# Gate weights stacked in one tile, and attention probabilities scaled on GpSimd instead of VectorE, in a one-core transformer layer

## What is computed

```python
def hybrid_mixer(x, w_in, conv_w, conv_b, ig_b, fg_b, ml_g, w_out, rel_table):
    proj = x @ w_in
    qa, ka, va, qk_m, vm, om, gates = jnp.split(proj, SPLITS, axis=-1)
    att = dilated_attention(heads(qa, 8), heads(ka, 8), heads(va, 8), rel_table)
    ig = (gates[..., :ML_HEADS] + ig_b).transpose(0, 2, 1)
    fg = (gates[..., ML_HEADS:] + fg_b).transpose(0, 2, 1)
    h = mlstm(heads(qm, 4), heads(km, 4), heads(vm, 4), ig, fg)
    ...
    return jnp.concatenate([att, h], axis=-1) @ w_out

# in the attention, per head and per block of 128 queries
logits = q @ k.T * ATT_HD ** -0.5 + bias      # masked outside the band
p = jnp.exp(logits - max(logits))
o = (p @ v) / sum(p)
```

## Time and profile before

| | |
|---|---|
| median of three runs | 1164.14 us |
| time of the profiled execution | 1164.95 us |
| its span, first to last instruction | 1163.0 us |
| TensorE busy | 99% |
| TensorE weight loads busy | 82% |
| VectorE busy | 49% |
| ScalarE busy | 36% |
| GpSimd busy | 3% |
| the chain that ended last | TensorE 97%, VectorE 2%, ScalarE 1% |
| TensorE's granted clock | 1.00 of full speed |

### The profile page before, as it was taken

One profiled execution on the slowest core, in us unless ns is written; L12 is line 12 of the kernel. 1 busy time (PEld: TensorE's weight loads), 2 busy tenths in 40 slices (PEclk: granted clock), 3 DMA queues, 4 the chain that ended last, 5 costly groups with the idle time before them and its releaser, 6 DMA issues.

```text
span 1163.0 us, 14755 instructions
## 1 busy us (share of the span) xinstructions
PE 1150.1 (99%) x5490; PEld 958.7 (82%) x5490; DVE 573.1 (49%) x930; ACT 422.2 (36%) x688; POOL 32.7 (3%) x49
## 2 busy tenths in 40 slices
PE   9999999999999999999999999999999999999997
PEld 8888888888888777888798888789888888888886
DVE  3533333343328588765884864456433333343325
ACT  4412212233225377643463454444221222233222
POOL 3000000000001011000000000000000000000000
PEclk9999999999999999999999999999999999999999
DMA  7532222232222222242243241232322222232211
GB/s 282 212 104 95 90 105 93 90 122 95 91 90 73 91 75 82 81 152 85 73 160 112 93 149 67 73 109 91 127 92 107 90 95 104 90 123 95 91 36 73
DMA packets 33563, 120.85 MB, mean 104 GB/s; under 512 B 3900, under 2 KB 3916, under 8 KB 33264
## 3 DMA queue, kind: packets, MB, share of 16 engines
q1 hardware_dynamic: 30528, 109.07, 27.3%
q0 software_dynamic: 2992, 11.19, 2.8%
HBM read 118.13 MB, written 2.11 MB: 103 GB/s over the span
## 4 chain that ended last, share of the span: by engine, by line
PE 97%; DVE 2%; ACT 1%; issue 0%; DVEq 0%; POOL 0%; POOLq 0%
PE ps L446 31%; PE ps L448 30%; PE ps L447 30%; PE ps L463 1%; PE ps L668 1%; PE ps L689 1%; PE ps L740 1%; PE ps L756 1%; PE ps L661 0%; PE ps L597 0%; PE ps L660 0%; DVE lg L1536 0%; PE ps L850 0%; DVE qs L1493 0%; DVE lg L1544 0%
## 5 line engine op out<-in xcount | busy, mean ns | idle before, releaser
L1336 DVE TENSOR_TENSOR wlo<-raw,whi 128x1024 fp32r<-128x1024 f32 x196 | 240.0, 1228 | 373.0 <-ACT whi L911 371.9
L446 PE MATMUL ps<-xth,whi 128*128 128x512 f32 (+1 forms) x924 | 355.0, 384 | 0.0
L448 PE MATMUL ps<-xth,wlo 128*128 128x512 f32 (+1 forms) x924 | 353.0, 382 | 0.0
L447 PE MATMUL ps<-xtl,whi 128*128 128x512 f32 (+1 forms) x924 | 352.9, 382 | 0.0
L911 ACT ACTIVATE whi<-raw 128x1024 fp32r<-128x1024 f32 (+1 forms) x204 | 207.1, 1037 | 152.1 <-PE ps L448 142.8
L448 PEld LDWEIGHTS ps<-xth,wlo 128*128 128x128 f32 x924 | 173.7, 188 | 34.1
L447 PEld LDWEIGHTS ps<-xtl,whi 128*128 128x128 f32 x924 | 173.8, 188 | 32.9
L446 PEld LDWEIGHTS ps<-xth,whi 128*128 128x128 f32 x924 | 173.8, 188 | 32.4
L446 PE MATMUL ps<-whi,hhi 128*128 128x512 f32 x480 | 187.8, 391 | 0.0
L448 PE MATMUL ps<-whi,hlo 128*128 128x512 f32 x480 | 186.9, 389 | 0.0
L447 PE MATMUL ps<-wlo,hhi 128*128 128x512 f32 x480 | 186.8, 389 | 0.0
(11 more groups left out here) (186 smaller groups left out, 997.2 us busy)
## 6 DMA issues: line engine op xcount, KB each, us to landing
raw<-in_units SPq DMA_DIRECT2D x204, 512.0 KB, 3.3
gb<-in_ln_g POOLq DMA_DIRECT2D x4, 512.0 KB, 3.9
gb<-in_ln_b POOLq DMA_DIRECT2D x4, 512.0 KB, 5.4
xn<-in_x POOLq DMA_DIRECT2D x4, 512.0 KB, 12.0
wb<-in_bias_by_key POOLq DMA_DIRECT2D x8, 256.0 KB, 3.0
out<-xn SPq DMA_DIRECT2D x8, 256.0 KB, 2.1
gsp<-g_rows POOLq DMA_DIRECT2D x1, 1024.0 KB, 4.8
memn<-in_mem_cols POOLq DMA_DIRECT2D x1, 1024.0 KB, 8.1
```

What stands on the lines that cost most here:

```text
L446: mm(dst, lh, rh, start=start, stop=False)
L447: mm(dst, lh, rl, start=False, stop=False)
L448: return mm(dst, ll, rh, start=False, stop=stop)
L1336: v.tensor_tensor(wlo[c % SPL][:, :], raw[c % RAW][:, :], whi[c % SPL][:, :].bitcast(F32), ALU.subtract).then_inc(lo_done, 1)
```

## The change

It has four parts. The gate weights go into one tile `wg` of 100 columns per block, high parts in columns 0 to 35 and low parts in columns 64 to 99, and the gate rows are formed with two matmuls per block (by `xh` and by `xl`) instead of three. The low part's rows come out as rows 64 to 99 of the same bank, so ScalarE copies two more 4 x 512 tiles out, and VectorE adds them in. The tile lies where `vx` lies, so `vx` is set to ones later, after the gate rows. The multiplication of the probabilities moves from VectorE to GpSimd, with a new semaphore `rinv_done` between the reciprocal and it. VectorE's `split(U_QK + 5)` moves behind the key's low parts. And `mem_key(0)` waits for the two pieces of `mtl` one by one.

```diff
-        wg_hi = at("wg_hi", [P, KT, GW], ...)
-        wg_lo = at("wg_lo", [P, KT, GW], ...)
+        wg = at("wg", [P, KT, 64 + GW], ar + 82 * KB, F32R)
...
@@ GpSimd
-            nc.gpsimd.memset(vx[:, :, :, :], 1.0).then_inc(pool_ok, 1)
+            nc.gpsimd.memset(wg[:, :, :].bitcast(F32), 0.0).then_inc(pool_ok, 1)
...
+            pool.wait_ge(grow_ready, 1)
+            nc.gpsimd.memset(vx[:, :, :, :], 1.0).then_inc(pool_ok, 1)
             pool.wait_ge(rows_done, 1)
             pool.dma_start(g_rows, grow[:, :]).then_inc(g_out, 16)
-            for h in range(2, AH):
-                bias_in(h)
-                bias_masked(h)
+
+            def scale_p(n):
+
+                w = (n % NB + 1) * P
+                pool.wait_ge(rinv_done, n + 1)
+                nc.gpsimd.tensor_scalar(lg[n % 3][:, 0:w], lg[n % 3][:, 0:w], rinv[:, n:n + 1], None, ALU.mult)\
+                    .then_inc(p_scaled, 1)
+
+            for n in range(NA):
+                if n % NB == NB - 1 and n // NB + 2 < AH:
+                    bias_in(n // NB + 2)
+                scale_p(n)
+                if n % NB == 0 and 2 <= n // NB + 1 < AH:
+                    bias_masked(n // NB + 1)
@@ TensorE
-                last = three(ps[1][0:GW, :], wg_hi[:, k, :], wg_lo[:, k, :], xh[:, k, :], xl[:, k, :], k == 0, k == KT - 1)
+                mm(ps[1][0:64 + GW, :], wg[:, k, :], xh[:, k, :], start=k == 0, stop=False)
+                last = mm(ps[1][0:64 + GW, :], wg[:, k, :], xl[:, k, :], start=False, stop=k == KT - 1)
...
-                    pe.wait_ge(mlo_done, 2)
...
-                cols_part(U_XK + t, ps[6 + t % 2][:, 0:MB * P], mth, mtl, 0, KT)
+                for half in range(2):
+                    if t == 0:
+                        pe.wait_ge(mlo_done, half + 1)
+                    cols_part(U_XK + t, ps[6 + t % 2][:, 0:MB * P], mth, mtl, 4 * half, 4 * half + 4)
@@ ScalarE
             fn(r_f[:, :], ps[1][32:GW, :], ACT.Copy).then_inc(f_ready, 1)
+            fn(r_e[:, :], ps[1][96:64 + GW, :], ACT.Copy).then_inc(f_ready, 1)
+            fn(r_a[:, :], ps[1][64:64 + MH, :], ACT.Copy).then_inc(f_ready, 1)
@@ VectorE
-            step.link(v.tensor_scalar(r_f[:, :], r_f[:, :], gbias[:, 1:2], None, ALU.add))
+            step.link(v.scalar_tensor_tensor(out=r_f[:, :], in0=r_f[:, :], scalar=gbias[:, 1:2], in1=r_e[:, :],
+                                             op0=ALU.add, op1=ALU.add))
...
-            split(U_QK + 5)
             k_lo(0, 0)
             k_lo(0, 1)
+            split(U_QK + 5)
...
-            def scale_p(n):
-                w = (n % NB + 1) * P
+            def invert_sum(n):
                 dve.wait_ge(p_done, n + 1)
-                step.link(v.reciprocal(rinv[:, n:n + 1], rsum[:, n:n + 1]))
-                v.tensor_scalar(lg[n % 3][:, 0:w], lg[n % 3][:, 0:w], rinv[:, n:n + 1], None, ALU.mult)\
-                    .then_inc(p_scaled, 1)
+                v.reciprocal(rinv[:, n:n + 1], rsum[:, n:n + 1]).then_inc(rinv_done, 1)
```

More of the change, by code:

```diff
@@ L213, in macaron_layer @@
         grow = at("grow", [MH, S], ar + 82 * KB + NB * MH * (P + 1) * 4)
-        wg_hi = at("wg_hi", [P, KT, GW], ar + 82 * KB + NB * MH * (P + 1) * 4, F32R)
-        wg_lo = at("wg_lo", [P, KT, GW], ar + 82 * KB + NB * MH * (P + 1) * 4 + KT * GW * 4, F32R)
+        wg = at("wg", [P, KT, 64 + GW], ar + 82 * KB, F32R)
         mth = at("mth", [P, KT, MB * P], ar + 32 * KB, F32R)
@@ L287, in macaron_layer @@
         tr_done = sem("tr_done")
+        rinv_done = sem("rinv_done")
         p_scaled = sem("p_scaled")
@@ L747, in numerators @@
                     pe.wait_ge(pj_ev, evacuated(G_VM + NB - 1))
-                    pe.wait_ge(pool_ok, 2)
+                    pe.wait_ge(pool_ok, 3)
                     pe.wait_ge(att_out, AH)
@@ L974, in ffn_up @@
                     act.wait_ge(small_in, 16 * SMALL)
-                    fn(wg_hi[:, :, :], wg_raw[:, :, :], ACT.Copy).then_inc(wg_hi_done, 1)
+                    act.wait_ge(pool_ok, 2)
+                    fn(wg[:, :, 0:GW], wg_raw[:, :, :], ACT.Copy).then_inc(wg_hi_done, 1)
                 with act.Fori(1, FT // 3) as i:
@@ L1154, in om_block @@
                 evacuate(G_OM + b, om[:, b, :], *ready, func=ACT.Tanh, scale=0.5)
-            act.wait_ge(pool_ok, 2)
+            act.wait_ge(pool_ok, 3)
             vm_block(0)
@@ L1409, in ffn_up @@
                     dve.wait_ge(wg_hi_done, 1)
-                    v.tensor_tensor(wg_lo[:, :, :], wg_raw[:, :, :], wg_hi[:, :, :].bitcast(F32), ALU.subtract)\
+                    v.tensor_tensor(wg[:, :, 64:], wg_raw[:, :, :], wg[:, :, 0:GW].bitcast(F32), ALU.subtract)\
                         .then_inc(wg_done, 1)
@@ L1506, in _ @@
             split(U_QK + 4)
-            dve.wait_ge(f_ready, 1)
-            step.link(v.tensor_scalar(r_f[:, :], r_f[:, :], gbias[:, 1:2], None, ALU.add))
+            dve.wait_ge(f_ready, 2)
+            step.link(v.scalar_tensor_tensor(out=r_f[:, :], in0=r_f[:, :], scalar=gbias[:, 1:2], in1=r_e[:, :],
+                                             op0=ALU.add, op1=ALU.add))
             v.scalar_tensor_tensor(out=r_e[:, :], in0=r_f[:, :], scalar=-1.0, in1=r_f[:, :],
                                    op0=ALU.mult, op1=ALU.max).then_inc(fabs_done, 1)
-            v.tensor_scalar(r_ig[:, :], ps[1][0:MH, :], gbias[:, 0:1], None, ALU.add).then_inc(ig_done, 1)
+            dve.wait_ge(f_ready, 3)
+            v.scalar_tensor_tensor(out=r_ig[:, :], in0=ps[1][0:MH, :], scalar=gbias[:, 0:1], in1=r_a[:, :],
+                                   op0=ALU.add, op1=ALU.add).then_inc(ig_done, 1)
             q_lo(0)
@@ L1584, in _ @@
                 if n >= 1:
-                    scale_p(n - 1)
+                    invert_sum(n - 1)
                 if n >= 2:
@@ L1602, in _ @@
                     conv(0)
-            scale_p(NA - 1)
+            invert_sum(NA - 1)
             silu(0)
```

## The result

| | before | changed |
|---|---|---|
| median of four runs | 1164.22 us | 1176.35 us |
| range of the runs | 1163.87 to 1164.82 | 1176.09 to 1177.01 |
| profiled execution | 1164.95 us | 1176.52 us |
| its span | 1163.0 us | 1174.7 us |

The ratio on record is 1.0107, with an interval of 1.0096 to 1.0119; the two medians alone give 1.0104. I had forecast 1165.2, in a range of 1161.0 to 1169.5. So the change costs 12.1 us where I had it cost 1, and the result lies outside the range.

The account below looks back on a forecast made before the run. TensorE, busy 99%, was taken as the bound. Stalls of 7.6 us less 2.69 before gave +4.9; less 3.77 saved, +1.1 on 1164.95, so 1166.05 profiled, 1165.2 as median; range 1161.0 to 1169.5.

Parts of the forecast that it names:

- the price of the multiplication: Attention, multiplication on GpSimd: 0.29, 0.42, 0.55 and 0.68 us for 128 to 512 columns, from two one-input operations.
- The upper end: GpSimd's multiplication at worst runs at the two-input addition's rate, 0.157 us + 2.2 ns per column.
- Rounds with n % 4 = 3: Attention, seven rounds of 384 columns: 2.47 us against own work of 2.07, a stall of 0.40 each, 2.8 us.
- the hop: From the reciprocal on VectorE to GpSimd's start: 0.20 us, with ends 0 and 0.31, entering 19 times.
- Rounds with n % 4 = 0: Attention, rounds of 512 columns: 2.34 us, under own work of 2.46, so no stall.
- the rival's 1171.1: Slower rival: GpSimd's multiplication runs at the addition's rate, price +5.9 us; chance 0.32 for all ends over 0.2% slower.
- Rounds with n % 4 = 1 and 2: Attention, where a table is added: 5.54 us against own work of 4.84, a stall of 0.70, six times, 4.2 us.
- The hold: GpSimd's table addition, started first, holds off VectorE's split of two SBUF inputs; next logits start at 4.23 instead of 3.41.
- Gate rows: Before the attention: 16 matmuls of 100 rows take 3.69 us instead of 24 in 5.54, saving 1.85 us.
- Memory keys: At the first memory key tile: TensorE's wait of 0.94 us for both pieces of `mtl` goes, all saved.
- First logits: Before the first logits: moving VectorE's split of 1.21 us removes TensorE's whole wait, saving 0.98 us.
- VectorE is behind in rounds 0 to 3: First head, where the moved split lands, and two rounds with query low parts: 0.6 us lost, between 0 and 1.21.

Follow-up runs that it names:

- The product form: Changed kernel with GpSimd's multiplication written as a product of two tensors, the second the reciprocal's column broadcast; 1166.01 us, ratio 1.0019 to the kernel before.

## Why the prediction was wrong

Against the steps of the prediction:

- **The failed step is the price of the multiplication:** "I take the first line, since the multiplication reads one tensor and a column". The two rows behind it were affine selections, another operation of the same engine. Instead of 0.29, 0.42, 0.55 and 0.68 us the rows after show 0.60, 0.92, 1.24 and 1.55 (1.62 in the mean). The upper end, the rate of the addition, was no end either: the real 2.5 ns per column lies above it. The claim that both one-input rows fit one fast line said only that this operation is fast, and two points fit any line.
- **Rounds with n % 4 = 3:** forecast 2.47 us, measured 3.10. Of the difference +0.69 is the multiplication (1.24 for 0.55), -0.11 the hop, +0.05 the reciprocal's start and the signal back. Seven stalls of 1.03 make 7.2, not 2.8.
- **Rounds with n % 4 = 0:** "No stall". Measured 2.85 against 2.46, seven times 0.39, so 2.7 us from nothing. The margin was 0.12 us, and I tested it only against a longer hop, not against the slow rate. By my own upper end the multiplication is 0.157 + 512 x 2.2 ns = 1.28 us, and the round 1.25 + 0.16 + 0.20 + 1.28 + 0.05 = 2.94. That is 0.48 too long, seven times 3.4 us, which the rival's 1171.1 left out. With it the rival's sum is 1174.5. This is the second fault, independent of the first.
- **That 1174.5 lies near the 1176.35 is partly luck.** The 1.25 us to the reciprocal is wrong for the changed kernel: there it starts 0.98 in (442.61 - 441.63). In the round of the earlier trace rows VectorE had come late to the logits: its `add_part` ended at 439.85 and they started at 439.88, while in the changed kernel it waited 1.10 us for TensorE there. With 1.25 and the real 1.55 the round would be 1.25 + 0.16 + 0.11 + 1.55 + 0.05 = 3.12, seven times 0.66, or 4.6 us instead of 2.7.
- **Rounds with n % 4 = 1 and 2:** the mechanism was right, order and hold included. A stall of 0.70 per table was forecast, 0.13 + 1.13 = 1.26 measured: +0.31 and +0.50 by the two multiplications, less 0.2 by two hops that were shorter; the last 0.05 is rounding and overlaps. Six times that is 7.6 us, not 4.2. The hold's share, 5.9 us, was shown by moving the addition.
- **The sum:** 7.2 + 2.7 + 7.6 = 17.5 us of stalls in rounds 3 to 29, where the trace has 78.33 - 60.75 = 17.58 and the forecast had 7.6. The difference of 10.0 is nearly the whole error of 11.2 us. Another 0.6 is the step from the profiled execution to the median: I took off 0.8, and in the changed kernel the two are 0.17 apart.
- **The hop:** 0.09 to 0.11 us from the reciprocal's end to GpSimd's start (433.86 to 433.95), not 0.20. It erred to the other side and hid some 2 us of the error.
- **Gate rows:** 1.86 us in the trace, 1.81 in the total of that part alone; 1.85 forecast. **Memory keys:** 1.05 in the trace and 0.73 in the total; 0.94 forecast. Both hold. **First logits:** the wait went as forecast. What "VectorE is behind in rounds 0 to 3" gives back is 0.78 us in one round with the multiplication on VectorE. In the changed kernel it doesn't show as a term of its own: the 17.5 us of the sum hold without the 0.6 that I put for it, and the first rounds lose 0.66 ahead of round 3.
- **The range** took in two thirds of a slow rate that itself was too low and priced without the rounds with n % 4 = 0. The chance of 0.32 for slower was too small for a price without any row of the operation.

The product form came out near the forecast (1166.0 us, 7.96 us of stalls), but this does not confirm its sum. With that form's rows (0.40, 0.61, 0.83 and 1.03 us) and a hop of 0.10 the forecast's working gives 4.1 us in rounds with n % 4 = 3, 4.8 for the tables and 0.9 in rounds with n % 4 = 0, 9.8 in all. Slower multiplications, a shorter hop and an earlier reciprocal offset each other.

What stays open: why the form with a scalar is slower than a product of two tensors. No run here looks inside GpSimd's instruction.

## What to carry to other kernels

An operation without a row of its own, on a slow engine and on the path, has no upper end until a row of that very form is seen. Here even the slowest rate of the engine's rows (2.2 ns per column) was too fast, so time the form by itself first. Then go through every round again whose margin was small, not only those that already stalled. Before elementwise work goes to GpSimd, count the latency and not its idle share, and look at what VectorE does with two SBUF inputs at the same moment. If a multiplication on GpSimd takes a scalar, try it as a product of two tensors, and tie background work on GpSimd to a place where VectorE doesn't need SBUF twice.

## What the runs showed of the hardware

- GpSimd on 128 x 512 float32 in SBUF: multiplication by a column 1.55 to 1.57 us undisturbed, by a constant 1.50, product of two tensors 1.04, product with a broadcast column 1.03, copy 0.61. The table's addition, whose two inputs are different tiles, takes 1.29.
- GpSimd starts 0.09 to 0.11 us after the reciprocal on VectorE ends (433.86 to 433.95, 442.77 to 442.88).
- The hold between VectorE's two-input split and GpSimd works both ways (2.21 for 1.23 us, 1.50 for 0.60). The loser ends 0.47 to 1.09 us after the winner, little less than its own 0.60 and 1.23. VectorE's multiplication by a column is held too (1.11 for 0.29).
- A matmul of 512 columns that fills 100 output rows starts 0.23 us after the one before, like those of 36 and 128 rows.
